# Wide FFNs in a two-block network: seven products in three shared PSUM banks, and where the modulation rows are summed

## The reference, cut to what matters

```
for l in range(2):
    mx, mz = nine vectors each: silu(c) @ w_mod[l] + b_mod[l], silu(c_ctx) @ w_mod[l] + b_mod[l]
    x = x + 0.5 * mx[2] * swiglu(modulate(rms_norm(x), mx[0], mx[1]), ffn1)      # FFN (l, 0)
    z = z + 0.5 * mz[2] * swiglu(modulate(rms_norm(z), mz[0], mz[1]), ffn1)
    ... token mixing with mx[3..5], mz[3..5] ...
    x = x + 0.5 * mx[8] * swiglu(modulate(rms_norm(x), mx[6], mx[7]), ffn2)      # FFN (l, 1)
    if l == 0: z = z + 0.5 * mz[8] * swiglu(modulate(rms_norm(z), mz[6], mz[7]), ffn2)
swiglu(h, w1, w3, w2) = (silu(h @ w1) * (h @ w3)) @ w2
```

## Time and profile before

| | |
|---|---|
| median of 3 runs | 3222.86 us (3222.63 to 3224.45) |
| profiled execution, span | 3223.4 us |
| TensorE matmuls busy | 3185.5 us, 99% |
| VectorE busy | 2125.0 us, 66% |
| ScalarE busy | 619.2 us, 19% |
| mean granted clock of TensorE | 0.997 |

### The profile page before, as it was taken

One profiled execution on the slowest core, in us unless ns is written; L12 is line 12 of the kernel. 1 busy time (PEld: TensorE's weight loads), 2 busy tenths in 40 slices (PEclk: granted clock), 3 DMA queues, 4 the chain that ended last, 5 costly groups with the idle time before them and its releaser, 6 DMA issues.

```text
span 3223.4 us, 44223 instructions
## 1 busy us (share of the span) xinstructions
PE 3185.5 (99%) x16992; PEld 2693.1 (84%) x16992; DVE 2125.0 (66%) x4261; ACT 619.2 (19%) x1354; POOL 123.6 (4%) x221
## 2 busy tenths in 40 slices
PE   8999999999999999999999989999999999999999
PEld 7888888988888889888885644888888888866999
DVE  6678657766786577775663773765757646556676
ACT  2121112121211121200003253100011000145221
POOL 0000000000000000100000010000000000001000
PEclk9999999999999999999999999999999999999999
DMA  6744677556446886543434121543425423232563
GB/s 191 189 112 153 222 227 226 193 161 166 112 144 219 240 233 202 156 140 103 137 99 120 40 53 53 157 145 106 128 85 157 137 66 98 80 112 53 142 175 129
DMA packets 587600, 456.12 MB, mean 142 GB/s; under 512 B 27792, under 2 KB 568880, under 8 KB 587008
## 3 DMA queue, kind: packets, MB, share of 16 engines
q1 hardware_dynamic: 564544, 373.65, 40.2%
q0 software_dynamic: 21376, 77.97, 7.8%
q10 hardware_dynamic: 1472, 1.68, 0.2%
HBM read 452.21 MB, written 1.05 MB: 141 GB/s over the span
## 4 chain that ended last, share of the span: by engine, by line
PE 97%; DVE 1%; ACT 1%; DMA 1%; issue 0%; POOL 0%; ACTq 0%; DVEq 0%; SPq 0%
PE psum L2258 38%; PE psum L2488 25%; PE psum L2511 12%; PE psum L2463 10%; PE psum L2265 3%; PE psum L2726 3%; PE psum L2702 1%; PE psum L2661 0%; PE psum L2599 0%; PE psum L2333 0%; POOL arena L1170 0%; PE psum L2537 0%; PE psum L2296 0%; PE psum L2419 0%; PE psum L2284 0%
## 5 line engine op out<-in xcount | busy, mean ns | idle before, releaser
L2258 PE MATMUL psum<-hh,ring 128*128 128x256 f32 (+1 forms) x4608 | 1076.4, 393 | 3.3 <-DVE hh L1745 3.0
L2258 PEld LDWEIGHTS psum<-hh,ring 128*128 128x128 f32 x4608 | 873.0, 191 | 181.1 <-issue 70.0
L2488 PE MATMUL psum<-hh,arena 128*128 128x256 f32 x1056 | 249.4, 379 | 0.0
L2488 PE MATMUL psum<-hh,ring 128*128 128x256 f32 x1056 | 242.0, 381 | 1.9 <-ACT hh L1505 1.9
L2488 PE MATMUL psum<-arena 128*128 128x256 f32 x1056 | 238.7, 379 | 0.0
L1816 DVE SCALAR_TENSOR_TENSOR arena<-arena,par 128x255 f32<-128x255 f32 (+14 forms) x480 | 225.1, 469 | 17.0
L2511 PE MATMUL psum<-arena 128*128 128x256 f32 x1056 | 231.8, 379 | 0.0
L2488 PEld LDWEIGHTS psum<-hh,ring 128*128 128x128 f32 x1056 | 198.7, 190 | 35.2 <-ACT hh L1505 4.8
L2488 PEld LDWEIGHTS psum<-arena 128*128 128x128 f32 x1056 | 200.6, 190 | 27.3
L2511 PEld LDWEIGHTS psum<-arena 128*128 128x128 f32 x1056 | 200.6, 190 | 27.3
L2488 PEld LDWEIGHTS psum<-hh,arena 128*128 128x128 f32 x1056 | 200.6, 190 | 27.3
(11 more groups left out here) (313 smaller groups left out, 3732.0 us busy)
## 6 DMA issues: line engine op xcount, KB each, us to landing
ring<-in_ffn_w SPq DMA_DIRECT2D x176, 512.0 KB, 5.2
ring<-in_w_in SPq DMA_DIRECT2D x54, 1024.0 KB, 5.3
ring<-in_w_up SPq DMA_DIRECT2D x88, 512.0 KB, 5.8
ring<-in_w_in SPq DMA_DIRECT2D x84, 512.0 KB, 5.3
mod_rows<-in_w_mod_rows POOLq DMA_DIRECT2D x72, 512.0 KB, 4.0
mod_rows<-in_w_mod_late_rows POOLq DMA_DIRECT2D x60, 512.0 KB, 4.3
ring<-in_ffn_w SPq DMA_DIRECT2D x16, 1536.0 KB, 6.8
ring<-in_ffn_w SPq DMA_DIRECT2D x16, 1280.0 KB, 6.0
```

What stands on the lines that cost most here:

```text
L2258: ins = mm(o[0:rows_, 0:T], w[:, k, c0:c0 + rows_], src[:, k, 0:T], start=(k == 0), stop=(k == kt - 1))
L2488: ins = mm(o[:, 0:S], lhs[:, k, :], rhs[:, k, :], start=(k == 0), stop=(k == half - 1))
```

## The change

1. The three 512-token FFNs take the shared-bank form: `uph`/`downh` with a width of 256 columns, four ScalarE copies and three VectorE adds a part. In part 0 the order of products is 0, 1, 4, 2, 5, 3, 6. The residual adds come straight after the adds that they need.
2. Of the four weight sums of a part, the two differences are made in one VectorE instruction of twice the length, with a broadcast operand. The input sums are made in another order (`h_t3` third).
3. The first network keeps 48 `modv` steps (its layer 1 has none left); the other 96 go to FFN (0,0), four after each part from part 1. Layer 1's turns move: turn 0 to FFN (0,1), turns 1 and 2 to FFN (1,0), with two rows at odd parts while two turns are left. `mod_r` now stands ahead of part 0, and for turn 2 behind the part in which turn 1 ends.
4. The 512-token squares of the next norm stay in `norm2`.

```diff
-FIRST_ORDER = (0, 1, 5, 4, 3, 2, 6)
+WIDE_FIRST = (0, 1, 4, 2, 5, 3, 6)
+TURNS_AT = {(0, 1): (0,), (1, 0): (1, 2)}
+EARLY_STEPS = 2 * 3 * KT
...
         norm(n)
         p.step("hsum", l, w)
+        turns = list(TURNS_AT.get((l, w), ()))
+        p.rows = 0
+        if turns:
+            p.step("mod_r", l, turns[0])
         for e, part in enumerate(parts):
             if e + 1 < len(parts):
                 p.step("wsum", l, w, *parts[e + 1])
             elif w == 1:
-                p.step("wsum", l + 1, 0, "up7", 0)
+                p.step("wsum", l + 1, 0, "uph", 0)
             name = (part[0], l, w, *part[1:])
-            p.parts[name] = len(p.parts)
-            p.step(*name)
-            for q in FIRST_ORDER if e == 0 else range(PROD):
-                p.job(*name, q, chunk=name)
+            p.half_part(name, WIDE_FIRST if e == 0 else HALF_ORDER)
             if e == 2:
                 mod_turn(p)
-            if e == 0:
-                p.rows = 0
-                p.step("mod_r", l, 2 * l + w)
-            else:
-                row_turn(p, 2 * l + w)
+            if e and (l, w) == (0, 0):
+                column_turn(p, 4, COLUMN_STEPS)
+            for _ in range(2 if len(turns) > 1 and e % 2 else 1):
+                if e and turns and row_turn(p, turns[0]):
+                    turns.pop(0)
+                    p.rows = 0
+                    if turns:
+                        p.step("mod_r", l, turns[0])
...
                     w = r[0]
                     if w == 0:
                         pool.wait_ge(row_summed, COLUMN_STEPS)
+                        produced(pool, job[("out", 0, KT - 1)])
                     else:
                         pool.wait_ge(late_row_summed, 2 * PACK * w)
-                        if w == 1:
-                            produced(pool, job[("out", 0, KT - 1)])
...
-                            added = KT * (ffn_at(l, 0) if n else ffn_at(l - 1, 1)) + KT // 2 + g // 2 + 1
-                            act.wait_ge(residual_top, added)
+                            before = (l, 0) if n else (l - 1, 1)
                             if g == KT - 1:
+                                act.wait_ge(half_added, top_added(("downh", *before, len(GROUPS) - 1, g // 2)))
                                 nc.scalar.activation(sq2[:, g, S:T], x[:, g, S:T], ACT.Square).then_inc(x2_squared, 1)
-                            if g % 2:
-                                act.wait_ge(residual_added, added)
+                            x_tile_added(act, *before, g)
...
-                        do(nc.scalar.activation(copy_of(name, q), bank(j)[:, 0:HALF], ACT.Copy), half_copied, 4 * n + m + 1)
+                        do(nc.scalar.activation(copy_of(name, q), bank(j)[:, 0:width(name)], ACT.Copy), half_copied, 4 * n + m + 1)
...
                     do(tt(s[:, 0], a21, a22, ALU.add))
-                    do(tt(s[:, 2], a11, a21, ALU.subtract))
                     do(tt(s[:, 1], s[:, 0], a11, ALU.subtract))
-                    do(tt(s[:, 3], a12, s[:, 1], ALU.subtract), wsum_ready, e + 1)
+                    n = s.shape[2]
+                    both = lower_quarters(name).rearrange("p m (e c) -> p m e c", e=2)
+                    twice = s[:, 1].rearrange("p m (e c) -> p m e c", e=1).to_broadcast([P, n, 2, P])
+                    do(tt(s[:, 2:4].rearrange("p e m c -> p m e c"), both, twice, ALU.subtract), wsum_ready, e + 1)
```

More of the change, by code:

```diff
@@ L265, in row_turn @@
             p.step("mod_w", DEPTH - 1, turn)
+    return p.rows == n
 def mod_turn(p):
@@ L494, in fast_ffn @@
         for g, (lo, hi) in enumerate(GROUPS):
-            parts += [("up7", i) for i in range(lo, hi)] + [("down7", g, j) for j in range(KT // 2)]
+            parts += [("uph", i) for i in range(lo, hi)] + [("downh", g, j) for j in range(KT // 2)]
         norm(n)
         p.step("hsum", l, w)
+        turns = list(TURNS_AT.get((l, w), ()))
+        p.rows = 0
+        if turns:
+            p.step("mod_r", l, turns[0])
         for e, part in enumerate(parts):
@@ L714, in plan_second @@
         if i == KT - 2:
-            p.step("wsum", l, 1, "uph" if last else "up7", 0)
+            p.step("wsum", l, 1, "uph", 0)
         p.step("out", l, i)
@@ L1058, in quarters, with lower_quarters @@
             return [w[:, :, u, P * e:P * (e + 1)] for e in range(2) for u in range(2)]
+        def lower_quarters(name):
+            w = weights(name)
+            if name[0] == "uph":
+                return w[:, KT // 2:KT, 0:2 * P]
+            return w.rearrange("p (m u) c -> p m u c", u=2)[:, :, 1, 0:2 * P]
         def weight_sums(name):
-            n = KT // 2 if name[0] in ("up7", "uph") else pieces(name)[0] // 2
+            n = KT // 2 if name[0] == "uph" else pieces(name)[0] // 2
             e = plan.parts[name] % 2
@@ L1065, in weight_sums, with wide, width @@
             return buf.rearrange("p (s m c) -> p s m c", s=4, m=n)
+        def wide(name):
+            return name[1:3] in ((0, 0), (0, 1), (1, 0))
+        def width(name):
+            return S if wide(name) else HALF
         def half_order(name):
-            return HALF_FIRST if name[0] == "uph" and name[-1] == 0 else HALF_ORDER
+            if name[0] == "uph" and name[-1] == 0:
+                return WIDE_FIRST if wide(name) else HALF_FIRST
+            return HALF_ORDER
         def half_copies(name):
@@ L1531, in _ @@
                                 nc.scalar.activation(squares(2 * l + 2)[:, g, :], x[:, g, 0:S], ACT.Square).then_inc(x_squared, 1)
[L1532 to L1543, removed]
                 elif kind == "gate_in":
@@ L1706, in push, with act_sums @@
                 ins.then_inc(vector_step, 1)
[L1708 to L1715, removed]
+            def act_sums(tiles, sums, n, m, before):
+                t1, t3, t4 = sums
+                half = tiles.shape[-1] // 2
+                b11, b12 = tiles[:, n - 1, 0:half], tiles[:, n - 1, half:]
+                b21, b22 = tiles[:, n, 0:half], tiles[:, n, half:]
+                do(tt(t1[:, n // 2, :], b12, b11, ALU.subtract))
+                do(tt(t3[:, n // 2, :], b22, b12, ALU.subtract))
+                do(tt(b12, b22, t1[:, n // 2, :], ALU.subtract))
+                do(tt(t4[:, n // 2, :], b21, b12, ALU.subtract), half_asum, before + m + 1)
             def scales_and_gates(l, lo, hi, cols):
@@ L1988, in _ @@
                     copied(dve, name, 0)
                     produced(dve, j2)
-                    free(tt(lead[:, 0:HALF], bank(j2)[:, 0:HALF], copy_of(name, 0), ALU.add), j2)
+                    free(tt(lead[:, 0:W], bank(j2)[:, 0:W], copy_of(name, 0), ALU.add), j2)
+                    if kind == "downh" and wide(name):
+                        do(residual(top[:, 0:W], lead[:, 0:W], 0, 0))
                     copied(dve, name, 3)
                     do(tt(low_sum, copy_of(name, 3), copy_of(name, 4), ALU.add))
+                    if kind == "downh" and wide(name):
+                        do(residual(low[:, W:], low_sum, 1, 1))
@@ L1993, in _ @@
                     produced(dve, j3)
-                    free(tt(lead[:, HALF:S], bank(j3)[:, 0:HALF], copy_of(name, 2), ALU.add), j3)
+                    free(tt(lead[:, W:], bank(j3)[:, 0:W], copy_of(name, 2), ALU.add), j3)
                     if kind == "uph":
                         i = r[1]
+                        tiles, at = (act7 if wide(name) else acth), group_tile(name, i)
                         dve.wait_ge(half_silu, up_names.index(name) + 1)
-                        do(tt(acth[:, i, HALF:S], low_sum, lead[:, HALF:S], ALU.mult))
+                        do(tt(tiles[:, at, W:], low_sum, lead[:, W:], ALU.mult))
@@ new lines, in _ @@
+                            sums = (a_t1, a_t3, a_t4) if wide(name) else (ah_t1, ah_t3, ah_t4)
+                            act_sums(tiles, sums, at, i // 2, sums_of(l, r[0]))
+                    else:
+                        if wide(name):
+                            do(residual(top[:, W:], lead[:, W:], 0, 1), half_added, top_added(name))
+                        else:
+                            do(residual(top, lead, 0, 0), half_added, top_added(name))
+                            do(residual(low[:, W:], low_sum, 1, 0))
+                        produced(dve, j4)
+                        free(residual(low[:, 0:W], bank(j4)[:, 0:W], 1, 0), j4)
@@ L2426, in _ @@
                     name = (kind, l, *r)
+                    W = width(name)
                     arrived(name)
@@ L2446, in _ @@
                                 pe.wait_ge(half_asum, sums_of(l, w) + hi)
-                        if kind == "uph" and i == 0 and q in sums:
-                            pe.wait_ge(hsum_ready, 4 * ffn_at(l, w) + sums[q])
-                        if kind == "downh" and q == 0:
+                        if kind == "uph" and i == 0 and q in waits:
+                            pe.wait_ge(hsum_ready, 4 * ffn_at(l, w) + waits[q])
+                        if kind == "downh" and q < 2:
```

243 lines of the change are left out of this document (71 added, 172 removed).

## The result

The changed kernel takes 3252.86 us (median of 4 runs, 3250.13 to 3254.63), the kernel before 3222.74 (4 runs): 30.1 us slower, a ratio of 1.0089 with a 95% interval of 1.0075 to 1.0103. The forecast was 3250, range 3240 to 3257.

What follows compares the result with a forecast made beforehand. TensorE, busy for 3185.5 of 3223.4 us, was taken as the bound. 3223.4 + 6.35 + 6.35 + 5.1 + 8.0 + 1.8 = 3251.0, less 0.5 to the median: 3250.4, given as 3250, range 3240 to 3257.

Steps and rivals of the forecast that it cites:

- stall at the entry of (0,1): Part 0 of FFN (0,1): TensorE waits for ScalarE's copy, queued behind the row load and Silu of `mod_r`; 6.35 us.
- stall at the entry of (1,0): Part 0 of FFN (1,0): the same wait for ScalarE's copy behind `mod_r`; 6.35 us again.
- stall inside (1,0): Part 17 of FFN (1,0): product 2 waits for the copy behind turn 2's row load and Silu; 5.1 us.
- clock after the three: After each of three stalls TensorE runs at half clock for 5.3 us, losing 2.65; 8.0 us in all.
- exits, three: Ends of the wide FFNs: ScalarE's squares for the next norm end later, +0.6 us each; 1.8 us.
- entry order and product 6, three: Part 0 of the wide FFNs: the third product needs `h_t1`, ready as TensorE arrives; 0 to 0.1 us, three times.
- last FFN (weight sums): Entry of the last FFN: the merged weight sum gains 0.2 us; together with the entry order taken as 0.
- -1.4 us bound: Exits of the wide FFNs: the figure if the squares went at their VectorE pace instead of costing 1.8 us.
- The moved steps and the adds: 96 modulation steps in FFN (0,0), VectorE keeping up at 92%: 0, bounded by +10; three adds instead of six: 0.
- (a): Rival: the stalls come but the clock keeps its upper level through some or all; 3242.5 with none lost; chance 0.12.
- (b): Rival: no stall, the row's Silu doesn't hold the copies; exits and last entry left, 3224.5 us; chance 0.13.
- (c): Rival: VectorE falls behind in the first FFN; 3260 us; chance 0.09, shared with loads that land late.

Runs made afterwards that it cites:

- Runs 1: Changed kernel with the first `mod_r` of FFNs (0,1) and (1,0) back behind part 0, turn 2's left in place: 3236.57 us, 12.4 above the kernel before.
- run 2: Changed kernel with `mod_r` cut in two: load issued as there, ScalarE's wait and Silu behind part 0, for turn 2 one part later: 3228.16 us.
- run 3: Changed kernel with the row load of (0,1) and (1,0) issued before GpSimd's scalings, ScalarE's wait and Silu still ahead of part 0: 3235.97 us.
- run 4: Kernel before with one edit, `mod_r` ahead of part 0 in all three wide FFNs: 3224.6 us, ratio 1.0001.
- run 6: run 2 with ScalarE squaring tiles 0 to 5 of the next norm inside the last down parts: 3226.58 us, 2.6 above the kernel before.
- run 7: run 2 with all 144 `modv` steps back in the first network, none in FFN (0,0): 3227.51 us, 3.5 above the kernel before.
- run 8: run 6 with the order 0, 1, 2, 4, 3, 5, 6 in part 0 of the wide FFNs: 3231.68 us, 7.7 above the kernel before.
- run 5: Changed kernel with the row load of (0,1) and (1,0) issued after four of GpSimd's eight scalings: 3243.93 us, 19.9 above the kernel before.

## Why the prediction was right

Point by point, with what was forecast and what the profiled execution shows:

| step | forecast, us | measured, us |
|---|---|---|
| stall at the entry of (0,1) | 6.35 | 5.93 |
| stall at the entry of (1,0) | 6.35 | 6.03 |
| stall inside (1,0) | 5.1 | 6.2 |
| clock after the three | 8.0 | 6.8 |
| exits, three | 1.8 | 1.7 |
| entry order and product 6, three | 0 | 3.6 |
| last FFN (weight sums) | -0.2, set against the row above | -0.3 |
| sum | 27.6 (the two rows above taken as 0) | 30.0 |

The measured terms add up to the 30.1 us between the medians. That the forecast came within 2.9 us of the time is in part luck: the entries were left out with 3.6 us and the third stall was priced 1.1 too low, while the clock was priced 1.2 too high and the first two stalls 0.7.

*The three stalls.* They came where forecast and by the mechanism forecast. Runs 1 and 2 take them away one after the other, and 17.7 and 26.1 of 30.1 us go; run 3 leaves the Silu in its place and shows that it is the wait; run 4 shows that the wait alone is free. The sizes are off by the load: at the entries it takes 4.5 and 4.6 us rather than the 4.9 of the earlier trace rows, in the middle of the FFN 5.7. The prediction took one duration for both places; why the third load was longer stays open.

*The clock.* Forecast from the one wait of 4.07 us in the earlier trace rows. It fell in all three stalls. The loss is 2.8, 2.5 and 1.5 us: it depends on how much of the 6.8 us at the lower level lies behind the end of the wait, and in the third most of it fell into the wait itself.

*The exits.* 0.57 us each against 0.6. That ScalarE ended last there was right for the changed kernel; run 6 shows that TensorE's own sums are next, 0.6 us behind, which the -1.4 us bound of the prediction missed.

*Entry order.* The one step that failed: "0 to 0.1 us, three times". The third product starts 0.27 us later, for the input sum, and the order 0, 1, 4, 2, 5, 3, 6 puts product 6 right behind product 3, whose copy it needs: 0.78 us at each entry. With 0.07 us more at each of the two restarts that makes 1.2. The prediction said that one other product lies between every pair, which holds for the usual order alone, and took the last FFN as its witness from 3022 on, past the row at 3018.74 that shows this wait. It is most of the 4 us by which run 2 stays behind the kernel before.

*The moved steps and the adds.* 0, and run 7 bears it out. VectorE's share in the up parts of (0,0) is 88%, "above 85%" as forecast; the working had said 92%.

*The rivals.* (a), stalls without the clock's loss, fell: the clock was lost in all three. (b), no stall, is what run 2 builds: 4.0 us above the kernel before, where the rival's 3224.5 is 1.6 above. It leaves out the entries, 3.6 us by the records, which more than covers the 2.4 between the two. (c), VectorE as the bound in the first FFN, didn't happen.

None of the other nine kernels is faster than the kernel before; run 6, without the three stalls and the late squares, is 2.6 us behind it, and its interval reaches just to no difference. Nothing in the profile says that the shared-bank form could win for 512 tokens: it saves VectorE work (1962.6 us busy instead of 2125.0), and VectorE wasn't the bound. Whether the freed PSUM banks could serve another change isn't tested.

## What to carry to other kernels

When a change makes the bounding engine depend on another engine's queue every few microseconds, walk through everything in that queue that waits for a DMA; a wait that cost nothing before becomes a stall of nearly its full length. Issue a load in one step and wait for it in another, a part later. And price a stall of the tensor engine with its clock: here each stall of 6 us took another 1.5 to 2.8. And where the first part runs in an order of its own, check every pair of dependent products in that order: here one pair stood side by side and cost 0.78 us each time.

## What the runs showed of the hardware that was not expected

The clock doesn't need a long wait to fall. It fell behind waits of 1.8 us in two of three places with the same wait (run 8) and behind one of 2.6 us but not one of 2.3 (run 5), each time for 3.4 us and only after work had resumed, by 0.4 and 0.5 us in run 8 and by 1.0 in run 5; behind the waits of about 6 us it fell every time, for 6.8 us (three in the changed kernel, one each in runs 1, 3 and 5). In the profiled executions of the other kernels, whose entries of the wide FFNs hold only idle pieces of 0.6 to 0.8 us, it didn't fall there. What decides between a fall and none behind the same wait is not shown.
